# A decoder layer in fp32: the value columns of the input projection computed as a unit of 7 products, and a new order in the first units and at the first border

## The reference, cut to what matters

```python
D_MODEL, SEQ, FFN_DIM = 2048, 256, 5632
IN_SPLITS = (512, 256, 64, 1024, 1024, 1024)     # c_q, c_kv, k_rope, q, k, v

h = swiglu(rms_norm(x, ffn1_pre_g), ffn1_w_gate, ffn1_w_up, ffn1_w_down)
x = x + 0.5 * rms_norm(h, ffn1_post_g)
u = rms_norm(x, mix_pre_g)
c_q, c_kv, k_rope, q_m, k_m, v_m = jnp.split(u @ w_in, cuts, axis=-1)
a = mla_attention(c_q, c_kv, k_rope, ...)        # 8 heads
m = moba_attention(q_m, k_m, v_m)                # 8 heads of 128; v_m is 1024 columns
y = jnp.concatenate([rms_norm(a, mla_out_g), rms_norm(m, moba_out_g)], axis=-1) @ w_out
x = x + rms_norm(y, mix_post_g)
h = swiglu(rms_norm(x, ffn2_pre_g), ffn2_w_gate, ffn2_w_up, ffn2_w_down)
x = x + 0.5 * rms_norm(h, ffn2_post_g)
```

## Time and profile before

| what | value |
|---|---|
| median of 3 runs | 1758.3 us (1758.13 to 1759.34) |
| the profiled execution's own time | 1758.18 us |
| its span | 1756.5 us |
| PE busy | 1737.1 us, 99% of the span |
| DVE busy | 1410.7 us, 80% |
| ACT busy | 1001.8 us, 57% |
| POOL busy | 65.3 us, 4% |
| mean granted TensorE clock | 0.998 of full speed |

### The profile page before, as it was taken

One profiled execution on the slowest core, in us unless ns is written; L12 is line 12 of the kernel. 1 busy time (PEld: TensorE's weight loads), 2 busy tenths in 40 slices (PEclk: granted clock), 3 DMA queues, 4 the chain that ended last, 5 costly groups with the idle time before them and its releaser, 6 DMA issues. The chain is left out here.

```text
span 1756.5 us, 21394 instructions
## 1 busy us (share of the span) xinstructions
PE 1737.1 (99%) x7968; PEld 1442.3 (82%) x7968; DVE 1410.7 (80%) x1284; ACT 1001.8 (57%) x979; POOL 65.3 (4%) x99
## 2 busy tenths in 40 slices
PE   9999999999999999999999999999999999999998
PEld 8788888888888888788888878788888888888886
DVE  7888888888888888765578558888888888888887
ACT  6666565555655654543347446555666666555563
POOL 1000000000000000010000000000000000000000
PEclk9999999999999999999999999999999999999999
DMA  9777777777766554355441546777777777666453
GB/s 386 237 257 259 256 256 239 239 239 248 245 234 222 184 215 176 147 219 189 174 162 54 187 171 260 263 240 241 249 249 241 239 246 251 254 232 238 174 191 114
DMA packets 58978, 389.75 MB, mean 222 GB/s; under 512 B 6432, under 2 KB 6688, under 8 KB 16160
## 3 DMA queue, kind: packets, MB, share of 16 engines
q1 hardware_dynamic: 52720, 344.77, 50.1%
q0 software_dynamic: 6048, 44.04, 13.2%
q10 hardware_dynamic: 144, 0.04, 0.0%
HBM read 384.63 MB, written 4.19 MB: 221 GB/s over the span
## 5 line engine op out<-in xcount | busy, mean ns | idle before, releaser
L2093 PE MATMUL banks<-w_hi,act_hi 128*128 128x512 f32 (+1 forms) x1088 | 424.7, 390 | 1.1 <-DVE act_lo L1355 1.1
L2095 PE MATMUL banks<-w_hi,act_lo 128*128 128x512 f32 (+1 forms) x1088 | 421.5, 387 | 0.0
L2094 PE MATMUL banks<-w_lo,act_hi 128*128 128x512 f32 (+1 forms) x1088 | 421.2, 387 | 0.0
L1385 DVE TENSOR_TENSOR op_lo<-quads,op_hi 128x2048 fp32r<-128x2048 f32 x140 | 318.5, 2288 | 43.2 <-ACT op_hi L918 42.8
L918 ACT ACTIVATE op_hi<-quads 128x2048 fp32r<-128x2048 f32 x140 | 266.8, 1919 | 53.3 <-PE banks L2095 21.1
L2287 PE MATMUL banks<-w_hi,hid_split 128*128 128x512 f32 x992 | 275.1, 389 | 0.5 <-DVE hid_split L1616 0.5
L1374 DVE TENSOR_TENSOR w_lo<-raw,w_hi 128x2048 fp32r<-128x2048 f32 x80 | 181.3, 2287 | 78.3 <-ACT w_hi L892 78.3
L1344 DVE TENSOR_TENSOR w_lo<-raw,w_hi 128x2048 fp32r<-128x2048 f32 (+3 forms) x67 | 143.8, 2147 | 121.6 <-ACT w_hi L843 121.6
L2093 PEld LDWEIGHTS banks<-w_hi,act_hi 128*128 128x128 f32 x1088 | 204.6, 188 | 42.1 <-issue 1.8
L2095 PEld LDWEIGHTS banks<-w_hi,act_lo 128*128 128x128 f32 x1088 | 204.4, 188 | 41.7
L2094 PEld LDWEIGHTS banks<-w_lo,act_hi 128*128 128x128 f32 x1088 | 204.6, 188 | 40.0
(11 more groups left out here) (209 smaller groups left out, 2329.8 us busy)
## 6 DMA issues: line engine op xcount, KB each, us to landing
raw<-in_weights SPq DMA_DIRECT2D x203, 1024.0 KB, 5.1
quads<-in_paired SPq DMA_DIRECT2D x80, 1024.0 KB, 10.7
quads<-in_paired POOLq DMA_DIRECT2D x40, 1024.0 KB, 8.5
raw<-in_paired SPq DMA_DIRECT2D x32, 768.0 KB, 5.9
rows<-in_x SPq DMA_DIRECT2D x4, 1024.0 KB, 10.9
raw<-in_weights SPq DMA_DIRECT2D x6, 512.0 KB, 3.5
gain_row<-in_post_gains SPq DMA_DIRECT2D x3, 1024.0 KB, 6.6
raw<-in_weights SPq DMA_DIRECT2D x4, 768.0 KB, 4.1
```

Source lines behind the costliest of these rows:

```text
L1385: nc.vector.tensor_tensor(op_lo[:, slot, :], op_raw(op), op_hi[slot][:, :], ALU.subtract)\
L2093: nc.tensor.matmul(out_ap, hi, rhs_hi, start=start, stop=False, skip_group_check=chain)
L2094: nc.tensor.matmul(out_ap, hi, rhs_lo, start=False, stop=False, skip_group_check=chain)
L2095: return nc.tensor.matmul(out_ap, lo, rhs_hi, start=False, stop=stop, skip_group_check=chain)
```

## The change: what it does

1. **Value columns.** The two value blocks become one unit of 7 products (stage MIX), with the two halves of the value columns as its near and far block. The weights of chunks 0 to 7 are laid out as four quarters, the others as four plain pieces. The unit's activations are made like those of a feed-forward stage: DVE joins high and low part (join_split), multiplies by the norm (norm_pairs, for which PE turns a row of norms, turn_rs) and makes the sums (sum_pairs). Operands lie in buffers that are free then: R22 and R21 are loaded into `gain_row`, R12 into `mix_normed`, and the latter only after its contents have been split (`pair_ready`).
2. **First units.** In unit 0 of GU1 and of GU2 DVE reads block 1's results (multiply_hidden) after splitting P6's operand instead of before sum3; the split of L4 moves behind the joins; PE turns the hidden block after P6 instead of before P7; ACT's copies move accordingly.
3. **First border.** For tile 1 the last piece of DOWN1 computes its first bank whole, then its second, and each is squared by itself.

```diff
@@ load_mix_unit (SP), new
+                sp.wait_ge(y_scaled, 4)
+                load_quad(MIX, v, R22)
+                load_plain(MIX, v, L1)
+                for n in range(RAW):
+                    load(piece(IN + 20 + n))
+                sp.wait_ge(lo_ready, IN + 21)
+                load_quad(MIX, v, R11)
+                sp.wait_ge(lo_ready, IN + 24)
+                load_plain(MIX, v, L2)
+                sp.wait_ge(pair_ready, ffn(MIX) + 1)
+                load_quad(MIX, v, R12)
+                sp.wait_ge(lo_ready, made(MIX, v.u, L1))
+                load_plain(MIX, v, L3)
...
@@ unit (DVE)
                 operand_low(stage, v, O_P7)
                 operand_low(stage, v, O_P6)
+                if v.first:
+                    multiply_hidden(stage, 1, 1)
                 plain_low(stage, v, L2)
                 plain_low(stage, v, L3)
                 operand_low(stage, v, O_P5)
                 operand_low(stage, v, O_P2)
-                plain_low(stage, v, L4)
+                if not v.first:
+                    plain_low(stage, v, L4)
...
                 join_part(part1, 0, banks[:, Y_BANK, :], ALU.subtract)
+                if v.first:
+                    plain_low(stage, v, L4)
                 operand_low(stage, v, O_P4)
@@ gate_up (DVE)
                 operand_low(stage, v, O_P3)
                 operand_low(stage, v, O_P1)
                 plain_low(stage, v, L1)
-                multiply_hidden(stage, 1, 1)
                 sum3(stage, v)
                 unit(stage, v)
@@ mix_unit (DVE), new
...
+                operand_low(MIX, v, O_P1)
+                take_low(piece(IN + 23))
+                dve.wait_ge(pair_hi_ready, 2 * ffn(MIX) + 2)
+                nc.vector.tensor_tensor(act_lo[:, 0:W_CHUNKS, :].rearrange("p c n -> p (c n)"),
+                                        mix_normed[:, :, :, :].rearrange("p a o n -> p (a o n)"),
+                                        act_hi[:, 0:W_CHUNKS, :].rearrange("p c n -> p (c n)"), ALU.subtract)\
+                  .then_inc(pair_ready, 1)
+                sum3(MIX, v)
+                plain_low(MIX, v, L1)
+                sum2(MIX, v)
+                rotate_qk(3, 1)
+                operand_low(MIX, v, O_P7)
+                operand_low(MIX, v, O_P6)
+                plain_low(MIX, v, L2)
...
@@ unit (PE)
                 product(stage, v, O_P3)
                 product(stage, v, O_P1)
                 plain_product(stage, v, L1)
-                turn_hidden(stage, v.u * 2 - 1)
+                if not v.first:
+                    turn_hidden(stage, v.u * 2 - 1)
                 product(stage, v, O_P7)
                 product(stage, v, O_P6)
+                if v.first:
+                    turn_hidden(stage, v.u * 2 - 1)
@@ mix_unit (PE), new; before it stand blocks of queries and keys as they were, and turn_rs(MIX) once
+                product(MIX, v, O_P3)
+                product(MIX, v, O_P1)
+                plain_product(MIX, v, L1)
+                product(MIX, v, O_P7)
+                product(MIX, v, O_P6)
+                turn_qk(3)
+                plain_product(MIX, v, L2)
+                product(MIX, v, O_P5)
+                plain_product(MIX, v, L3)
+                product(MIX, v, O_P2)
+                product(MIX, v, O_P4)
+                plain_product(MIX, v, L4)
@@ down_piece (PE), the last piece of DOWN1 for tile 1
+                        for k in range(2):
+                            for j in range(2):
...
+                            mm.then_inc(piece_used if k else near_bank_done, 1)
@@ square_end (ACT), new, instead of square_down(DOWN1, 1)
+                square(banks[:, b:b + 2, :].rearrange("p b n -> p (b n)"), junk[:, 0:D // 2], 0, 1)
+                act.wait_ge(near_bank_done, 1)
+                square(banks[:, down_banks(1, 1), :], junk[:, 0:BANK], 1, 1)
+                act.wait_ge(piece_used, stage + DP)
+                square(banks[:, down_banks(1, 1) + 1, :], junk[:, 0:BANK], 1, 2)
```

More of the change, by code:

```diff
@@ L404, in turned_chunk, with quad_raw @@
             return xT[:, c, :] if turn == 0 else turn_at(turn, c // 4, c % 4)
-        def quad_raw(q):
+        def quad_raw(stage, q):
+            if stage == MIX and q == R11:
+                return raw[:, 0, :]
+            if stage == MIX and q == R12:
+                return mix_normed[:, :, :, :].rearrange("p a o n -> p (a o n)")
+            if stage == MIX:
+                return gain_row[:, :]
             return quads[:, q, :]
@@ L1881, in mix_in @@
                 dve.wait_ge(tab_scaled, 2)
-                with dve.Fori(0, 2) as n:
-                    for e in range(2):
-                        for i in range(4):
-                            take_low(piece(IN + 12 + 4 * e + i, n, 8))
-                            if i == 1:
-                                rotate_qk(2 * n + e, e)
-                take_low(piece(IN + 28))
-                take_low(piece(IN + 29))
-                scale_v1(0, 0)
-                take_low(piece(IN + 30))
-                take_low(piece(IN + 31))
+                dve.wait_ge(rs_ready, rs_of(R_KV))
@@ new lines, in mix_in @@
+                for t in range(TILES):
+                    nc.vector.tensor_scalar(tab_q[:, t, :], tab[:, t, MOBA_TAB:], rs[:, R_Q, t:t + 1],
+                                            None, ALU.mult).then_inc(tab_scaled, 1)
+                spread_rs(MIX)
+                take_low(piece(IN + 12))
+                take_low(piece(IN + 13))
+                rotate_qk(0, 0)
+                take_low(piece(IN + 14))
+                join_split(MIX)
+                take_low(piece(IN + 15))
+                norm_pairs(MIX)
@@ L2084, in _ @@
             gate_up(GU2)
[L2085 removed]
+            down_proj(GU2, DOWN2, 27, 3)
             finish()
@@ L2162, in plain_product @@
                 turn = plain_turn(v, k)
-                blocks = B_GU1 if stage == GU1 else B_GU2
+                blocks = {GU1: B_GU1, MIX: B_UQ - 3, GU2: B_GU2}[stage]
                 pe.wait_ge(lo_ready, made(stage, v.u, k))
@@ L2281, in down_piece @@
                         pe.wait_ge(end_added, added + (4 if t else 2))
+                    if stage == DOWN1 and n == DP - 1 and t:
+                        for k in range(2):
+                            for j in range(2):
+                                hi = hid_split[:, pc.split, 0, j, tile_of(t)]
+                                lo = hid_split[:, pc.split, 1, j, tile_of(t)]
+                                for lhs, rhs in ((hi, rhs_hi), (hi, rhs_lo), (lo, rhs_hi)):
+                                    mm = nc.tensor.matmul(banks[:, b + k, :], lhs, rhs[:, j, quarter(k)],
+                                                          start=False, stop=True, skip_group_check=True)
+                            mm.then_inc(piece_used if k else near_bank_done, 1)
+                        continue
                     for j in range(2):
@@ L2624, in lay_out_weights @@
     put(IN + 8, cut_up(w_in[:, rest:], 4, BANK))
+    values = w_in[:, rest + 2 * HEADS * HD:].reshape(DC, P, 2, BANK)
+    near, far = values[:, :, 0], values[:, :, 1]
+    stream[MIX + 8:MIX + 8 + PLAIN] = [np.concatenate(list(part), axis=1)
+                                       for part in (far[8:12], far[12:16], near[8:12], near[12:16])]
+    stream[MIX + 8 + PLAIN:UQ] = 0.0
+    paired[MIX_QUADS:] = [np.concatenate([b[2 * a + k] for a in range(PAIRS)], axis=1)
+                          for k in range(2) for b in (near, far)]
     put(UQ, cut_up(w["mla_w_uq"][0], QC, UQ_WIDTH))
```

319 lines of the change are left out of this document (231 added, 88 removed).

## The result

The changed kernel takes **1776.25 us** (median of 5 runs, 1774.92 to 1777.8) against 1758.7 us of the kernel before, measured beside it (5 runs, 1758.13 to 1759.46): a ratio of 1.0102, 95% interval 1.009 to 1.0113. It is slower by 1.0%. The forecast was 1775.0 us. The profiled execution took 1776.25 us with a span of 1774.6 us, 18.1 us more than before.

A forecast was written before the change was run, and what follows sets the result against it. PE's own instructions were taken to set the time. Waits and value unit +13.2, clock +3.4, first border -0.4, and +0.4 gave +16.6 us on 1758.3: 1774.9, stated as 1775 us; 8-in-10 range 1769.5 to 1783.

The forecast's parts named there:

- The reading's place: First units of GU1 and GU2: PE waits 8.5 us before L1 for DVE's later reading of block 1's banks.
- The old waits that vanish: First units: PE's earlier short waits between L1 and L4 go, -1.85 us in GU1 and -1.95 in GU2.
- The clock in the first units: Behind each long gap before L1, PE's clock falls to half: 1.7 us for each, +3.4 us together.
- Part 1: Value unit: 12 fewer matmuls -2.72, turn_rs +0.45, wait for P7's operand behind R12's load +2.7; net +0.4 us.
- the rival that is late and slow: R12 lands after 8.5 us, P7's gap brings half clock, first units pay 1.5 stretches each: 1781.8 us, chance 0.19.
- The first border: Border after DOWN1: the smaller last square lets DVE's scaling and PE's transposes start earlier, -0.4 us, bounds 0 and -1.
- The second border: No term in the sum; the prediction only noted the clock at half for 3.4 us there in the earlier trace.
- without the clock's loss: Rival: the gaps before L1 come but PE finds the full clock behind them; 1771.6 us, chance 0.16.
- The faster case: Rival: in the first units DVE leads enough that its reading doesn't hold PE before L1; 1754.5 us, chance 0.05.

The follow-up runs named there:

- the reading halfway: Changed kernel with DVE's reading of block 1's results in the first units moved between sum2 and the split of P7: 1769.34 us, ratio 1.0057.

## Why the prediction was right, and where its terms were off

- **The reading's place (+8.5 us of wait twice): right.** DVE read at 67.11 where 67.2 was forecast, PE started L1 at 68.13 where 68.1 was; the wait was 8.47 and 8.48 us. What decided was to count the four instructions now ahead of the reading and to see in the earlier trace rows that it had been ready only 0.46 us before PE needed it. Two runs, one with the call put back and one with it alone moved, show it from both sides.
- **The old waits that vanish (-1.85 and -1.95): right.** By the trace GU1's first unit lost 8.8 us = 8.47 + 2.1 (half clock) - 1.8; the waits before P7 and the 0.7 us before turn_hidden are gone. The first units as before, in GU2, had only 0.8 us of such waits, so their size is not a fixed one.
- **The clock in the first units (+3.4): right in kind, a little small.** L1 lasted 2.1 and 1.8 us longer, 3.9 in sum, where one stretch of 3.4 us under load was taken for each. The run with matmuls in the gaps shows that it is the clock: there L1 takes 5.60 us.
- **Part 1 (+0.4): the step that failed.** The sizes behind it held: 4.9 us for R12's load where 5.1 was taken, a gap of 2.42 us where 2.7 was, +0.44 for turn_rs where 0.45 was. By the Trainium skill, "DMA: Bandwidth & Descriptors", in the section on the anatomy of one DMA of GpSimd's path, a load of 1 MB would be 4.4 us, an estimate by that page; this load is issued by SP, and the trace has 4.9, nearer to the median of the rows. But I gave the half clock only to the two long gaps and kept it for P7's gap in the rival that is late and slow. The gap of 2.42 us brought it too: P7 took 1.7 us longer. Part 1 cost +0.44 + 1.6 = +2.0 us. Filling the gap, or taking it away, removed this part.
- **The first border (-0.4): right**, -0.35 measured from the last piece to the first matmul behind it.
- **The second border (0): off by -0.8 us**, not through the change. The clock had fallen there in the execution of before and did not in that of the changed kernel. That this made up for half of part 1's error is luck.

The sum of the trace: 8.8 - 0.35 + 0.44 + 1.6 - 0.8 + 8.5 = +18.2 us, which agrees with the spans' 18.1; the forecast had +16.6. Part 1's missing 1.7 and the second border's -0.8 are most of the difference. By the medians, 1776.25 - 1758.7 = 17.55 us.

The rivals: without the clock's loss (1771.6) fell by the windows. The faster case (1754.5) fell by the first wait. The late and slow one (1781.8) was right on P7's clock and wrong on R12's landing; it gave the first units 5.1 us for the clock, where L1 lost 3.9.

What stays open: the run with matmuls in the gaps was 1.3 us above its expectation in the median, and the two places where its trace loses time (0.8 and 0.9 us) are known for that one execution alone. The profiled executions show where the half-clock stretches fell in one run of each kernel; how often they fall at a border in the other runs isn't shown. Whether the first border's edit gives anything in the median wasn't tried alone.

## What to carry to other kernels

An instruction that frees a buffer for the engine that sets the time belongs ahead of all work that this engine doesn't need at once; four DVE instructions put before two small readings cost 1% of the kernel's time here. Before moving such a call, find in the timeline how long its result lies ready before it is needed; the time of what is put ahead (8.9 us here), less that slack (0.46 us here), is the new wait. And a saving of matmuls counts only once its operands are on time: the unit of 7 products gained nothing until work that nobody waited for was moved behind its operands.

## What the runs showed of the hardware that I had not expected

- A gap of PE cost more than its length by 1.7 us (gap of 2.4), 2.8 and 2.3 us (two gaps of 4.0) and 2.1 and 1.8 us (two gaps of 8.5; 2.5 and 1.9 us in the run with the reading alone moved): twice the gap did not cost more behind it.
- The gap of 2.3 to 2.4 us before P7 stands in five traces, and in all five the granted clock fell to half behind it, for 3 to 4 us.
- Matmuls whose output nobody uses, put into the gap, kept the granted clock at 1.00 behind it and made P7 1.6 us and L1 1.9 us shorter. The gap of the reading itself isn't shortened by them.
- At the two borders the clock fell in some executions and in others not, with the same instructions. At the second border, the same in all kernels, it fell in two of the ten traces (before, and P7's gap filled) and cost 0.8 us. At the first border in its new order it fell in two of eight (the reading halfway, the matmuls in the gaps) and cost 0.7 and 0.9 us; in its old order it fell in the run with the reading alone moved, for 7 us and at a cost of 2.0 us, and not in the kernel before. The Trainium skill, "TensorE: Matmul & The Clock Gate", Part 1, says that the chip's sampling runs free of the kernel; this agrees with it. A comparison of two single traces is therefore uncertain by 0.7 to 2.0 us for each border.
